# The first expert layer of a two-layer block, from four blocks of tokens per head to two passes of two blocks

## What is computed

```
q   = (x @ w_q).reshape(n, 8 heads, 2, 128)
s   = einsum('nhpd,hpkd->nhpk', q, sub_keys)          # 2 x 128 scores per token and head
sv, si = top_k(s, 16)
cand   = sv[:, :, 0, :, None] + sv[:, :, 1, None, :]   # 256 candidates
top_s, pos = top_k(cand, 16)
eidx   = the 16 expert numbers that belong to pos      # of 16384
gate   = softmax(top_s)
act    = gelu(einsum('nd,nhkd->nhk', x, u[eidx]))
y      = einsum('nhk,nhkd->nd', gate * act, v[eidx])   # sum over 8 heads and 16 picks
x      = x + mod[5] * y
```

## Time and profile before

| what | value |
|---|---|
| median of 3 executions | 2931.4 us (2931.21 to 2931.75) |
| the profiled execution | 2930.89 us |
| its span, first to last instruction | 2929.1 us |
| mean granted TensorE clock | 0.965 |
| PE busy | 2446.0 us (84%) |
| DVE busy | 1784.6 us (61%) |
| ACT busy | 1036.8 us (35%) |
| POOL busy | 835.6 us (29%) |
| moved by DMA | 917.02 MB, mean 313 GB/s |

### The profile page before, as it was taken

The page is one execution under the profiler, slowest core; times in us unless marked ns, Lnnn a source line. Parts: engine busy times, 40 slices in busy tenths (PEclk is TensorE's granted clock), DMA queues, the critical chain, the costliest instruction groups (busy, mean ns, idle before and its releaser), DMA issues. The chain is left out here.

```text
span 2929.1 us, 22782 instructions
## 1 busy us (share of the span) xinstructions
PE 2446.0 (84%) x6582; PEld 1076.7 (37%) x6582; DVE 1784.6 (61%) x4142; ACT 1036.8 (35%) x2897; POOL 835.6 (29%) x791
## 2 busy tenths in 40 slices
PE   6989986878788787988888777799787888888776
PEld 2533333323333232323333222347575333333222
DVE  3956733767676667666666675213445666666765
ACT  1022212444444444444434443211312443444443
POOL 0000000544444344443444442000102434434441
PEclk8999998999999999999999999899888999999999
DMA  7523311999999999999999997224005999999995
GB/s 294 180 102 144 144 29 49 413 421 421 421 421 420 421 420 421 421 421 421 421 421 421 421 420 303 72 72 134 10 29 203 420 420 420 420 421 421 421 421 246
DMA packets 133388, 917.02 MB, mean 313 GB/s; under 512 B 15248, under 2 KB 17296, under 8 KB 31504
## 3 DMA queue, kind: packets, MB, share of 16 engines
q0 software_dynamic: 111168, 813.74, 67.0%
q1 hardware_dynamic: 22096, 101.83, 9.7%
HBM read 914.47 MB, written 1.05 MB: 313 GB/s over the span
## 5 line engine op out<-in xcount | busy, mean ns | idle before, releaser
L908 PE MATMUL pY<-uv,diag 128*128 128x512 f32 x3072 | 1485.5, 619 | 350.5 <-ACT diag L965 349.8
L1097 DVE SCALAR_TENSOR_TENSOR uv<-uv,H 128x1024 f32<-128x1024 f32 x768 | 941.1, 1225 | 633.2 <-DMA uv<-uv_dram,idx 632.7
L839 POOL DMA_INDIRECT uv<-uv_dram,idx x768 | 812.1, 1057 | 1556.6 <-PE pY L908 1061.6
L908 PEld LDWEIGHTS pY<-uv,diag 128*128 128x128 f32 x3072 | 548.8, 192 | 1264.4 <-ACT diag L965 760.5
L957 ACT ACTIVATE gelu<-dots 128x1 f32<-128x1 f32 x768 | 155.5, 202 | 1023.7 <-DVE uv L1097 1023.2
L965 ACT ACTIVATE diag<-cst,coef 128x128 f32<-128x128 f32 x768 | 308.2, 401 | 72.6 <-PE pY L908 2.2
L961 ACT ACTIVATE coef<-gelu,gate 128x1 f32<-128x1 f32 x768 | 226.2, 295 | 27.8
L852 PE MATMUL pq<-h2T,wring 128*128 128x512 f32 (+1 forms) x512 | 172.9, 492 | 20.3 <-PEq L236 20.3
L120 PE MATMUL plh<-h1T,wring 128*128 128x512 f32 (+1 forms) x512 | 168.3, 492 | 12.9 <-PEq L236 12.9
L852 PEld LDWEIGHTS pq<-h2T,wring 128*128 128x128 f32 x512 | 98.8, 194 | 95.0 <-issue 88.8
L120 PEld LDWEIGHTS plh<-h1T,wring 128*128 128x128 f32 x512 | 98.3, 192 | 83.2 <-issue 76.6
(11 more groups left out here) (237 smaller groups left out, 1846.5 us busy)
## 6 DMA issues: line engine op xcount, KB each, us to landing
aw<-ada_w_dram SPq DMA_DIRECT2D x20, 2048.0 KB, 8.4
wring<-peer_q_dram SPq DMA_DIRECT2D x32, 512.0 KB, 10.4
uv<-uv_dram,idx POOLq DMA_INDIRECT x768, 25.2
aw<-ada_w_dram POOLq DMA_DIRECT2D x4, 2048.0 KB, 8.9
wring<-hg_zz_dram SPq DMA_DIRECT2D x16, 512.0 KB, 3.6
wring<-hg_qg_dram SPq DMA_DIRECT2D x16, 512.0 KB, 3.6
wring<-w_in_dram SPq DMA_DIRECT2D x12, 512.0 KB, 4.3
wring<-w_out_dram SPq DMA_DIRECT2D x8, 512.0 KB, 3.6
```

The source lines that it names most:

```text
L839: nc.gpsimd.indirect_dma_start(out=uv[:, n % SLOTS, :], out_offset=None, in_=t[f"uv{l}"], in_offset=bass.IndirectOffsetOnAxis(ap=idx[:, s, ...
L908: last = nc.tensor.matmul(pY[:, s % 2, half * 512:(half + 1) * 512], diag[:, n % DIAGS, :], uv[:, n % SLOTS, D + half * 512:D + (half + 1) ...
L1097: v.scalar_tensor_tensor(out=uv[:, j, 0:D], in0=uv[:, j, 0:D], scalar=1.0, in1=H2[:, b, :], op0=ALU.mult, op1=ALU.mult, accum_out=dots[:, ...
```

## The change

Layer 0 becomes one stream of 16 heads: eight heads on the 256 tokens of `ctx` and then the same eight heads on the 256 tokens of `x`, two blocks each. Layer 1 is one pass of eight heads as before. Both layers now look two heads ahead. The tiles of `w_q` of layer 0 are listed twice in the ring's order, and its keys are loaded per head of the stream, so both come twice from memory. Each block has its own half of `pY`, in which PE accumulates over all eight heads of a pass (128 picks); `Y` holds two blocks instead of four and is written once per block by a copy (`take`). ACT copies both halves of a query at once, PSUM has a separate tile `pt` for turning back, and `turn_back` and `residual` work in two halves of four transposes and four updates each. The norm and the `H2` transposes still cover all 512 columns at the layer's start.

```diff
-        lin = [("w_in", 12), ("w_out", 8), ("peer_q0", 16),
+        lin = [("w_in", 12), ("w_out", 8), ("peer_q0", 16), ("peer_q0", 16),
                ("hg_zz", 16), ("hg_qg", 16), ("hg_out", 8), ("peer_q1", 16)]
...
+            passes = ([(2, T), (3, 0)], [(7, 0)])[l]
...
-    blocks = (4, 2)[l]
+    BLOCKS = T // P
+    blocks = BLOCKS * len(passes)
     cols = blocks * P
-    steps = blocks * HEADS
+    heads = HEADS * len(passes)
+    steps = heads * BLOCKS
+    PASS = HEADS * BLOCKS
...
-    HEADS_AHEAD = 1 if blocks == 4 else 2
-    SBUFS = HEADS_AHEAD
+    HEADS_AHEAD = 2
...
-        pY = ps(f"pY{l}", [P, 2, D], c)
-        pq = ps(f"pq{l}", [P, 2, 512], c)
-        psc = ps(f"psc{l}", [P, blocks, 2, P], c)
+        pY = ps(f"pY{l}", [P, BLOCKS, D], c)
+        pq = ps(f"pq{l}", [P, 2, T], c)
+        psc = ps(f"psc{l}", [P, BLOCKS, 2, P], c)
+        pt = ps(f"pt{l}", [P, 4, P], c)
...
         def _(sp):
-            for h in range(HEADS):
+            for h in range(heads):
                 if h >= 2:
                     sp.wait_ge(s_sc, h - 1)
-                sp.dma_start(keys[:, h % 2], t[f"keys{l}"][:, 2 * h:2 * h + 2, :]).then_inc(s_keys[h % 2], 16)
+                k0 = 2 * (h % HEADS)
+                sp.dma_start(keys[:, h % 2], t[f"keys{l}"][:, k0:k0 + 2, :]).then_inc(s_keys[h % 2], 16)
                 if h >= 2:
-                    for j in (2 * h, 2 * h + 1):
-                        load_tile(sp, f"peer_q{l}", j, g0 + j)
-            lin_ahead(sp, which)
+                    for i in two:
+                        load_tile(sp, f"peer_q{l}", k0 + i, tile(h) + i)
+            lin_ahead(sp, passes[-1][0])
...
                 for k in range(KT):
-                    last = nc.tensor.matmul(pq[:, i, 0:cols], wring[:, (g0 + j) % RING, k * P:(k + 1) * P], hT[:, k, :],
+                    last = nc.tensor.matmul(pq[:, i, :], wring[:, g % RING, k * P:(k + 1) * P], hT[:, k, own:own + T],
                                             start=(k == 0), stop=(k == KT - 1))
...
-                if k == 0 and s >= 2:
-                    pe.wait_ge(s_added, s - 1)
-                for half in range(2):
-                    last = nc.tensor.matmul(pY[:, s % 2, half * 512:(half + 1) * 512], diag[:, n % DIAGS, :],
+                if k == 0 and s >= PASS and s % PASS < BLOCKS:
+                    pe.wait_ge(s_copied, s // PASS * BLOCKS - BLOCKS + b + 1)
+                for half in two:
+                    last = nc.tensor.matmul(pY[:, b, half * 512:(half + 1) * 512], diag[:, n % DIAGS, :],
                                             uv[:, n % SLOTS, D + half * 512:D + (half + 1) * 512],
-                                            start=(k == 0), stop=(k == TOPK - 1), skip_group_check=True)
+                                            start=(s % PASS < BLOCKS and k == 0),
+                                            stop=(s % PASS >= PASS - BLOCKS and k == TOPK - 1), skip_group_check=True)
...
-            def add(s):
-
-                b = s % blocks
-                dve.wait_ge(s_pick, (s + 1) * TOPK)
-                if s < blocks:
-                    v.tensor_copy(Y[:, b, :], pY[:, s % 2, :]).then_inc(s_added, 1)
-                else:
-                    v.tensor_tensor(Y[:, b, :], Y[:, b, :], pY[:, s % 2, :], ALU.add).then_inc(s_added, 1)
...
+            def take(s):
+
+                dve.wait_ge(s_pick, (s + 1) * TOPK)
+                v.tensor_copy(Y[:, s % BLOCKS, :], pY[:, s % BLOCKS, :]).then_inc(s_copied, 1)
...
+            def residual(s, half):
+
+                block_no = s // PASS * BLOCKS + s % BLOCKS
+                dve.wait_ge(s_turned, 2 * block_no + half + 1)
+                span = tokens(s // BLOCKS, s % BLOCKS)
+                who = span.start // T
+                for k in range(4):
+                    last = v.scalar_tensor_tensor(out=xT[:, 4 * half + k, span], in0=pt[:, k, :],
+                                                  scalar=modT[:, l, 5, 4 * half + k, who:who + 1],
+                                                  in1=xT[:, 4 * half + k, span], op0=ALU.mult, op1=ALU.add)
                 last.then_inc(s_out, 1)
...
-                    if k == 8 and s >= 1:
-                        add(s - 1)
-                    if k == 15 and h == HEADS - 1 and b >= 1:
-                        residual(b - 1)
-            add(steps - 1)
-            residual(blocks - 1)
+                    if k == 8 and ends:
+                        take(done)
+                    if k == 12 and ends:
+                        residual(done, 0)
+                    if k == 15 and ends:
+                        residual(done, 1)
+            take(steps - 1)
+            residual(steps - 1, 0)
+            residual(steps - 1, 1)
```

More of the change, by code:

```diff
@@ L82, in build @@
         acc_free = sem("acc_free")
-        lin = [("w_in", 12), ("w_out", 8), ("peer_q0", 16),
+        lin = [("w_in", 12), ("w_out", 8), ("peer_q0", 16), ("peer_q0", 16),
                ("hg_zz", 16), ("hg_qg", 16), ("hg_out", 8), ("peer_q1", 16)]
[L85 to L89, removed]
+        first = [sum(n for _, n in lin[:i]) for i in range(len(lin))]
         def load_tile(sp, name, i, g):
@@ L99, in lin_ahead @@
             if which + 1 < len(lin):
-                name, n = lin[which]
                 for j in range(RING):
-                    load_tile(sp, lin[which + 1][0], j, first[name] + n + j)
+                    load_tile(sp, lin[which + 1][0], j, first[which + 1] + j)
         def lin_loads(sp, which):
@@ L107, in lin_loads @@
             for i in range(RING, n):
-                load_tile(sp, name, i, first[name] + i)
+                load_tile(sp, name, i, first[which] + i)
             lin_ahead(sp, which)
@@ L113, in lin_matmuls @@
             name, n = lin[which]
-            g0 = first[name]
+            g0 = first[which]
             for i in range(n):
@@ L135, in lin_done @@
             name, n = lin[which]
-            eng.wait_ge(acc_free, RING + first[name] + (tiles or n))
+            eng.wait_ge(acc_free, RING + first[which] + (tiles or n))
         s_xT, s_const, s_cond, s_sc, s_mod = sem("s_xT"), sem("s_const"), sem("s_cond"), sem("s_sc"), sem("s_mod")
@@ L861, in scores @@
                     pe.wait_ge(s_sce, h)
-                for b in range(blocks):
-                    for i in range(2):
+                for b in range(BLOCKS):
+                    for i in two:
                         last = nc.tensor.matmul(psc[:, b, i, :], qT[:, i, b * P:(b + 1) * P], keys[:, h % 2, i, :],
@@ L866, in scores, with turn_back @@
                 last.then_inc(s_sc, 1)
[L868 to L874, removed]
+            def turn_back(s, half):
+                block_no = s // PASS * BLOCKS + s % BLOCKS
+                pe.wait_ge(s_copied, block_no + 1)
+                if 2 * block_no + half >= 1:
+                    pe.wait_ge(s_out, 2 * block_no + half)
+                for k in range(4):
+                    at = (4 * half + k) * P
+                    last = nc.tensor.transpose(pt[:, k, :], Y[:, s % BLOCKS, at:at + P], ident)
                 last.then_inc(s_turned, 1)
@@ L901, in _ @@
                         scores(h + HEADS_AHEAD)
-                if h == HEADS - 1 and b >= 1 and k == 13:
-                    turn_back(b - 1)
+                done = s - 1
+                if done >= 0 and done % PASS >= PASS - BLOCKS:
+                    if k == 10:
+                        turn_back(done, 0)
+                    if k == 13:
+                        turn_back(done, 1)
                 pe.wait_ge(s_diag, n + 1)
-                if k == 0 and s >= 2:
-                    pe.wait_ge(s_added, s - 1)
@@ L911, in _, with queries @@
                 last.then_inc(s_pick, 1)
-            turn_back(blocks - 1)
+            turn_back(steps - 1, 0)
+            turn_back(steps - 1, 1)
         @block.scalar
         def _(act):
-            def queries(h, i):
-                act.wait_ge(acc_ready, g0 + 2 * h + i + 1)
+            def queries(h):
+                act.wait_ge(acc_ready, tile(h) + 2)
                 if h >= 1:
                     act.wait_ge(s_sc, h)
-                nc.scalar.copy(qT[:, i, :], pq[:, i, 0:cols]).then_inc(acc_free, 1)
+                nc.scalar.copy(qT[:], pq[:]).then_inc(acc_free, 2)
@@ L946, in _ @@
                 s, k = divmod(n, TOPK)
[L947 to L950, removed]
+                h, b = place(s)
+                if h + HEADS_AHEAD < heads:
                     if (b, k) == (1, 0):
-                        queries(h + HEADS_AHEAD, 1)
+                        queries(h + HEADS_AHEAD)
                     if (b, k) == (1, 8):
@@ L1089, in _ @@
             for s in range(steps):
-                h, b = divmod(s, blocks)
+                h, b = place(s)
+                own = s // PASS * BLOCKS + b
+                done = s - 1
+                ends = done >= 0 and done % PASS >= PASS - BLOCKS
                 for k in range(TOPK):
```

90 lines of the change are left out of this document (49 added, 41 removed).

## The result

The changed kernel took 2952.11 us (median of 4, 2951.15 to 2952.31) against 2931.31 us for the kernel before, timed beside it: 1.0070 times as long, 95% interval 1.0057 to 1.0083. It is 20.8 us slower. The forecast was 2948 with a range of 2941 to 2954: the sign and the mechanism held, and the sum was 4 us short.

The account below looks back on a forecast made before the run. The prediction took the DMA engines to bound the gather stages; second loads 23.3, earlier first gather -8.2, instructions 1.0 and ends 0.7 gave +16.8 us on 2931.4, forecast as 2948 us, range 2941 to 2954.

Parts of the forecast that it names:

- What bounds the kernel: Gather stages of both layers: the DMA engines, at a share of 1.01 and 421 GB/s, set the time.
- The second load: Layer 0's gathers: 9.44 MB of weights and keys loaded again cost 23.3 us, bounds 22.4 to 24.4.
- the instruction term: Layer 0: fetching about a tenth more PE instructions adds 1.0 us, bounds 0 to 1.5.
- hidden: Rival, layer 0's gathers: second loads cost less than about 1 us a head, giving 2924 us; 3 in 100.
- half hidden: Rival, layer 0's gathers: a head's loads cost 1.2 to 1.7 us, giving 2934 to 2938 us; 5 in 100.
- memory side: Rival, layer 0's gathers: tiles read between random rows cost 3.4 us a head, giving 2953 us; 6 in 100.
- the prediction's worry about one DMA engine behind the rest: Gathers: one of 16 DMA engines lags and sets the pace, so price bytes by landings, not only mean bandwidth.
- The earlier first gather: Layer 0's start: first gather 20.7 us after the first key issue instead of 28.9, gaining 8.2 us.
- the slack of some 15 us: Layer 0's start: 12 slots hold 29.9 us of gathers, so some 15 us remain before anything is lost.
- The work per step: Gathers of both layers: DVE loses about 34 and 17 us of work, worth nothing; new waits cost nothing.
- The two ends: End of each layer, closing in halves: 0.3 us longer each, 0.7 us together, bounds 0 to 1.2.
- the joint copy of both query halves: Layer 0's start: copying both halves takes 0.59 us against 0.37 for layer 1's second copy, making 20.7 us.

Follow-up runs that it names:

- e1: Changed kernel with the 16 second-pass weight tiles loading only 16 of 1024 columns, all waits and issues kept: 2931.12 us.
- e2: Kernel before, with 16 more tile loads and 8 more key loads (9.44 MB) in layer 0 that nothing reads: 2954.24 us.
- e7: Kernel before, with the next linear layer's four tiles loaded only when all but the last of layer 0's picks are used: 2923.46 us.
- e6: Kernel before, with head 0's queries and scores made for the first 128 columns ahead, in both layers: 2916.89 us.
- e3: Changed kernel with the old sums back: PSUM holds one step and DVE copies or adds each step to Y: 2951.95 us.
- e4: Changed kernel with turn_back and residual again in one piece of eight transposes and eight updates: 2947.82 us.
- e5: Kernel before, with head 0's queries and scores made for columns 0 to 255 first, in layer 0 only: 2926.85 us.
- e8: Kernel before, with the first 128 columns of head 0 ahead in both layers and the late load of the next tiles: 2913.55 us.

## Why the prediction was right, and where it was short

**What bounds the kernel** was right: 1.01 and 421 GB/s held through both passes, and e1 took most of the price away and e2 put all of it on the old order, without touching anything else. No run tells apart whether the DMA engines, a port or the memory set the 421 GB/s.

**The second load.** Forecast 23.3 us, bounds 22.4 to 24.4, and 1.0 more for instructions. Measured 23.6 for both in the changed kernel (1336.37 - 1312.74) and 23.5 in e2, which adds loads and no PE instructions. The load term held; the instruction term was worth about nothing. At 2.9 us a head the rivals "hidden" (under 1), "half hidden" (1.2 to 1.7) and "memory side" (3.4) are out. The tile's 1.2 us in e1 and e7 is 512 KB at 421 GB/s (1.25 us), so bytes at the mean bandwidth were a fair price, and the prediction's worry about one DMA engine behind the rest didn't matter for it. The 358 GB/s that the Trainium skill gives as the limit of memory per core in "DMA: Bandwidth & Descriptors", section "Where 436 GB/s comes from", is a stack's 716 GB/s divided between two cores. By it the loads would be 26.4 us, an estimate; here, where one core ran alone, the runs measured 23.5.

**The earlier first gather.** Forecast -8.2, measured -8.1. A side reason was off: I put the first dot product 12 us behind the first gather, and it was 9.25. It didn't matter, as the slack of some 15 us was there, and e6 used 20 of the 29.9 us without a gap.

**The work per step.** Forecast nothing, and e3 shows nothing. The DMA share over the change of passes (1150 to 1240 us, in windows of 20 to 50 us) stayed at 1.01 to 1.02, so the new waits held up no transfer.

**The two ends.** Forecast 0.7, measured 0.6 + 0.5 = 1.1, all of it the halves by e4.

**What the sum left out.** The parts that I summed came to +16.8 by forecast and -8.1 + 23.6 + 1.1 = +16.6 by measurement. The medians lie 20.8 us apart, which is above the +13.9 to +20.1 of the forecast's own bounds; the range took it in only by the 2 or 3 us that it allowed for what no row shows. That it was enough is in part luck. The other 3.4 us of the 20.0 between the spans are pieces for which the sum had no term: the longer norms and what lies between, +1.0 and +1.0; layer 1's gathers, +0.8; its start, +0.2; and +0.3 before anything changed. The 0.2 was to be had: the joint copy of both query halves, which I charged to layer 0, is in layer 1 too. The longer final norm goes with PE's clock. Rows of the norm's matmuls, first before, then after:

```profile
2912.45 5.41 PE L275 MATMUL nf_pn<-nf_sqb,ones 128*128 128x256 f32 x16 [2.96 <-ACT nf_sqb L264]
...
2912.40:2917.90 5.50, 5.41 (x16) 4.14 (x16) 0.01 (x1) 3.42 (x8) 0.00 (x0) 0.69 0.00 0
```

```profile
2931.42 6.41 PE L270 MATMUL nf_pn<-nf_sqb,ones 128*128 128x256 f32 x16 [1.93 <-ACT nf_sqb L259]
...
2931.40:2937.90 6.50, 6.41 (x16) 4.88 (x16) 0.03 (x1) 3.39 (x8) 0.00 (x0) 0.58 0.00 0
```

The same 16 records took 1.0 us longer, at a mean granted clock of 0.58 instead of 0.69: more of them ran at the lower of its two levels (0.5 and 1.0 in these rows). That it isn't the new end of the layer is shown by e5 and e6, which have the old end and took 6.24 and 6.49 us for them, while e2 took 5.41. What decides it was not found. Layer 1's +0.8 was seen in e1, e3 and e4 too (662.8 to 663.0) and not in e2 and e5 to e8 (662.1 to 662.4), so it goes with the new form of `peer_phase`. Nearly all of it is there by the ninth dot product of layer 1 (29.65 us after the first gather instead of 28.93; 29.58 in e1, 29.63 in e4), so it lies in the layer's start; which part of the new code makes it was not tried.

## What to carry to other kernels

Where, as here, the DMA engines show a share of 1.01 through a whole stage, look first at three numbers: when the first transfer starts (8.1 us here), how many bytes ride along (23.6 us), and what follows the last (1.1 us). Work taken off an engine that waits for landings gave nothing: 51 us of DVE's adds, taken out or put back, didn't show. Before a loop is cut into passes, count what each pass must load again, and look whether the head start that it brings can be had alone: splitting off only the first block's work of the first head, in both layers, gave 15 us (e6) where the passes lost 21. A load issued for later wasn't hidden by being early: in e2 nothing ever read the loads, and each head's cost 2.9 us. It was hidden where the DMA engines had nothing else to do: e7's four tiles in the norm, and head 2's tiles ahead of the first gather.

## What the runs showed of the hardware that I had not expected

Sections with the same code differ between profiled executions of kernels that differ elsewhere: up to the first key issue 481.3 to 484.0 us, and the recurrence 360.9 to 364.8 us. In the recurrence the time of PE moves along: busy 331.1 us before, 329.3 in e1, 327.6 in e7. One kernel's own executions differ as much: 2929.2 to 2933.3 in 13 and 2929.3 to 2935.2 in 18 of the kernel before, and 2948.1 to 2952.9 in e3's four, although the changed kernel's four lie within 1.2 us. So a difference of medians below some 4 us between two kernels needs its place in the timeline before it is believed. And in each last stretch of layer 0's gathers looked at, before and after, the mean DMA share fell to 0.07 for about 10 us with landings still awaited; that one DMA engine of 16 is behind is inferred from that number, not seen by itself.
